# Pattern B's scores from stacked hi/lo operands in two fp32r passes, with a second key set where pattern C's position tables stand

## The chip, the cores and the metric

One core of one Trainium2 chip. The time is the device time of one execution in microseconds; the time before is the median of 3 runs.

## What is computed

A two-layer encoder trunk over 512 tokens of width 1024. In each layer one combined projection feeds four token mixers (A: windowed attention, B: differential attention, C: dilated attention, D: latent attention) and four gates; the gated branches are summed, projected and added, then comes a gated MLP. The change is in B, cut from the reference:

```python
def differential_attention(b_q, b_k, b_v, pos, q_norm, k_norm, lam_q1, ...):
    q = rms_norm(b_q.reshape(b, s, 2, B_HEADS, HEAD_DIM), q_norm)
    k = rms_norm(b_k.reshape(b, s, 2, B_HEADS, HEAD_DIM), k_norm)
    v = b_v.reshape(b, s, B_HEADS, B_V_DIM)
    ...
        sc = jnp.einsum('bqmhd,bsmhd->bmhqs', qblk, k, preferred_element_type=jnp.float32) * scale
        dist = jnp.abs(pblk[:, :, None] - posf[:, None, :])
        sc = sc - slopes[None, None, :, :, None, None] * dist[:, :, None, None]
        a = jax.nn.softmax(sc, axis=-1)
        a = a[:, 0] - lam[None, :, None, None] * a[:, 1]
        return jnp.einsum('bhqs,bshv->bqhv', a.astype(v.dtype), v, ...)
```

There are 4 heads with 2 maps each (head size 64), so with 4 query tiles of 128 tokens 32 score tiles of 128 x 512 in a layer.

## The kernel before, in words

Everything stays in SBUF; weights stream in through a two-deep buffer `raw` and are split by ScalarE into a high part `wh` (fp32r, L961) and by VectorE into the rest `wl` (L1481). Each dense product of TensorE is three fp32r matmuls, high by high, low by high, high by low (L579), six to a step. ORDER lists the dense blocks with their number of steps; it is the clock of the whole program. WINDOW gives each attention pattern a span of that clock, `slots` divides it into n + 4 slots, and every engine's program is a merge (`together`) of streams that yield the time at which they want to issue. So the order on each engine is fixed when the program is built, and semaphores do the rest.

B's window holds 32 steps in 36 slots between the blocks br0a and gate1b, so that of four slots three hold one dense step and one holds two. In a slot TensorE does, in this order: in odd slots the transposes of a mixed probability tile into bank TA (through L614), in even slots the product with the values into O1 (L850), and the scores of the step into the single bank S1 (L859). VectorE adds the bias and takes the minimum (L2023), ScalarE takes the exponential (L1366), VectorE mixes the two maps of a head (L2007, L2009, L2011), and the transposed tile is copied out of TA half by ScalarE (L1360), half by VectorE (L2017). TensorE may write the scores of the next step when L2023 has read S1.

The stationary operand of a score is `q_pad`, 128 rows of which 64 are the head's and 64 are zero; ScalarE copies q into it in eight pieces for a window, two copies each (L1307, `tiles_of`), pieces 0 and 1 before the window, piece p (2 to 7) after step 4p-4. The product is a plain fp32 one with kT.

Before the window, B's q and k are normalised and transposed, four tiles each: TensorE transposes a tile of 128 tokens into bank TD (`turn`), and `half_out` empties it, two of four column blocks by ScalarE (L1180 for k), two by VectorE (L1870). A's last steps run meanwhile, and their copy out of TA stands behind it on VectorE (L1978), A's output by heads is L2075, and its split for block br0a is ScalarE's L1189 and VectorE's L1878.

Pattern A does its scores in another way (`stacks_of_a`, `stacks`, L815): operands `q_two` with the high part of q in one half of the rows and a copy of it in the other, against keys kept twice. ScalarE writes the high part (L1324), VectorE copies it to the other rows (L1955) and writes the rest, q minus its high part (L1957).

`near` (second half) and `bias_c12` hold C's tables of position distances and masks; they are built once at the start and read in C's windows of both layers.

## Time and profile before

| | |
|---|---|
| median of 3 runs | 2708.42 us (2707.78 to 2709.2) |
| the profiled execution, time | 2709.8 us |
| its span, first to last instruction | 2708.0 us |
| granted TensorE clock, mean | 0.998 |
| TensorE busy | 2629.4 us, 97% |
| VectorE busy | 1639.1 us, 61% |
| ScalarE busy | 1231.4 us, 45% |
| B's score matmuls (L859), records and busy | 128, 66.4 us |
| DMA | 225.28 MB, mean 83 GB/s |

A plain fp32 matmul shows as two records. Matmuls are pipelined and their ends are modelled, so lengths of single ones overlap the next; distances between starts are the safer measure. ScalarE's and VectorE's lengths are their own.

### The profile page before, as it was taken

The numbers are of one execution on the slowest core, as the hardware profiler recorded it, in microseconds if no ns is written. First come the engines' busy times: TensorE is split into PE (matmuls) and PEld (weight loads), VectorE is DVE, ScalarE is ACT, GpSimd is POOL, SyncE is SP. The second block draws the span as 40 slices with busy tenths as digits, with TensorE's granted clock in tenths as the row PEclk, the third lists the DMA queues.
The fourth block names the chain that finished last, engine by engine and source line by source line (L and its number), as shares of the span: only waits on it lengthen the run. The fifth ranks groups of instructions, "written<-read, shape, count | busy, mean of one in ns | idle before, by whom it ended". The sixth has DMA issues, their size and how long they took to land. (4 is left out here: it accounts for less than half of the span.)

```text
span 2708.0 us, 36172 instructions
## 1 busy us (share of the span) xinstructions
PE 2629.4 (97%) x12982; PEld 2205.3 (81%) x12982; DVE 1639.1 (61%) x3432; ACT 1231.4 (45%) x2514; POOL 1.5 (0%) x6
## 2 busy tenths in 40 slices
PE   7999999999999999999999999999999999999999
PEld 6999987778877778888779998877788777888887
DVE  6554577545666647676664546775356566485665
ACT  5655545444544334333354555544445443443332
POOL 0000000000000000000000000000000000000000
PEclk9999999999999999999999999999999999999999
DMA  5212223222121332332332122221221213333332
GB/s 184 70 55 79 81 65 92 57 77 72 55 78 48 104 100 88 95 103 88 102 117 71 47 87 74 80 86 55 71 78 56 78 47 109 94 94 101 95 100 94
DMA packets 143874, 225.28 MB, mean 83 GB/s; under 512 B 15046, under 2 KB 69458, under 8 KB 142802
## 3 DMA queue, kind: packets, MB, share of 16 engines
q1 hardware_dynamic: 135842, 201.85, 24.8%
q10 hardware_dynamic: 7856, 21.12, 2.1%
q8 instruction: 106, 1.74, 0.3%
q14 instruction: 70, 0.57, 0.1%
HBM read 210.29 MB, written 12.65 MB: 82 GB/s over the span
## 5 line engine op out<-in xcount | busy, mean ns | idle before, releaser
L1481 DVE TENSOR_TENSOR s_wl<-s_raw,s_wh 128x1024 fp32r<-128x1024 f32 (+2 forms) x376 | 453.2, 1206 | 297.9 <-ACT s_wh L961 297.7
L961 ACT ACTIVATE s_wh<-s_raw 128x1024 fp32r<-128x1024 f32 (+2 forms) x376 | 392.0, 1043 | 396.6 <-PE bank L579 298.3
L579 PE MATMUL bank<-s_hTh,s_wh 128*128 128x512 f32 x1216 | 520.9, 428 | 1.6 <-DVE s_work L1839 1.6
L579 PE MATMUL bank<-s_hTh,s_wl 128*128 128x512 f32 x1216 | 474.7, 390 | 0.0
L579 PE MATMUL bank<-s_hTl,s_wh 128*128 128x512 f32 x1216 | 473.9, 390 | 0.0
L579 PE MATMUL bank<-s_wh,s_hTh 128*128 128x512 f32 (+1 forms) x1088 | 458.1, 421 | 4.5 <-DVE s_early L1621 3.4
L579 PE MATMUL bank<-s_wh,s_hTl 128*128 128x512 f32 (+1 forms) x1088 | 426.2, 392 | 0.0
L579 PE MATMUL bank<-s_wl,s_hTh 128*128 128x512 f32 (+1 forms) x1088 | 425.8, 391 | 0.0
L579 PEld LDWEIGHTS bank<-s_hTh,s_wh 128*128 128x128 f32 x1216 | 228.6, 188 | 69.8 <-issue 23.6
L1278 ACT ACTIVATE s_work<-s_work,s_stat 128x128 f32<-128x128 f32 (+3 forms) x320 | 167.5, 524 | 257.5 <-DVE s_work L2053 113.6
L579 PEld LDWEIGHTS bank<-s_hTl,s_wh 128*128 128x128 f32 x1216 | 228.9, 188 | 66.4 <-issue 24.4
L579 PEld LDWEIGHTS bank<-s_wh,s_hTh 128*128 128x128 f32 x1088 | 251.6, 231 | 34.6 <-issue 4.1
L579 PEld LDWEIGHTS bank<-s_wh,s_hTl 128*128 128x128 f32 x1088 | 251.7, 231 | 26.6
L579 PEld LDWEIGHTS bank<-s_wl,s_hTh 128*128 128x128 f32 x1088 | 253.4, 233 | 22.5 <-issue 0.5
L579 PEld LDWEIGHTS bank<-s_hTh,s_wl 128*128 128x128 f32 x1216 | 228.2, 188 | 49.1
L614 PE MATMUL bank<-s_consts,s_work 128*128 128x128 f32 (+1 forms) x1432 | 216.4, 273 | 16.0 <-DVE s_gTl L1878 8.9
L614 PEld LDWEIGHTS bank<-s_consts,s_work 128*128 128x128 f32 (+1 forms) x1432 | 172.6, 139 | 70.7 <-issue 34.3
L1978 DVE COPY s_work<-bank 128x128 f32<-128x128 f32 (+1 forms) x224 | 77.4, 345 | 207.4 <-PE bank L614 98.1
L579 PE MATMUL bank<-s_wh,s_gTh 128*128 128x512 f32 (+1 forms) x432 | 167.4, 387 | 5.6 <-ACT s_work L990 5.2
L579 PE MATMUL bank<-s_wl,s_gTh 128*128 128x512 f32 (+1 forms) x432 | 166.3, 385 | 0.0
L579 PE MATMUL bank<-s_wh,s_gTl 128*128 128x512 f32 (+1 forms) x432 | 166.2, 385 | 0.0
L579 PE MATMUL bank<-s_gTh,s_wh 128*128 128x512 f32 x256 | 111.4, 435 | 5.9 <-DVE s_gTl L1878 3.0
(202 smaller groups left out, 3408.4 us busy)
## 6 DMA issues: line engine op xcount, KB each, us to landing
s_raw<-in_w_in SPq DMA_DIRECT2D x168, 512.0 KB, 3.6
s_raw<-in_ffn_w_up SPq DMA_DIRECT2D x176, 256.0 KB, 3.1
s_raw<-in_ffn_w_down SPq DMA_DIRECT2D x44, 512.0 KB, 3.7
s_raw<-in_w_branch SPq DMA_DIRECT2D x32, 512.0 KB, 3.7
s_raw<-in_w_o SPq DMA_DIRECT2D x16, 512.0 KB, 3.7
x_keep<-s_work ACTq DMA_DIRECT2D x2, 2048.0 KB, 11.2
s_raw<-in_w_in SPq DMA_DIRECT2D x16, 256.0 KB, 3.0
gate_keep<-s_early ACTq DMA_DIRECT2D x4, 1024.0 KB, 4.3
```

Source lines behind the costliest of these rows:

```text
L579: last = mm(PJ[b][:, 0:width], st, mv, start=i == 0 and n == 1, stop=i == ntiles - 1 and n == 3 * chunks)
L614: last = nc.tensor.transpose(dst[0:m, (at + n) * P:(at + n) * P + k], src, ident[0:k, 0:k])
L961: a(wh[:, k % 3, 0:n], raw[:, s, 0:n], ACT.Copy).then_inc(*hi_split.up(own))
L1278: a(probs[:, u % 2, x0:x0 + w], scores[:, u % 2, x0:x0 + w], ACT.Exp, scale=-1.0, bias=stat[:, mins, c:c + 1], accum_out=stat[:, sums, c:c ...
L1481: v.tensor_tensor(wl[:, k % 3, 0:n], raw[:, k % 2, 0:n], wh[:, k % 3, 0:n].bitcast(F32), ALU.subtract).then_inc(*tile_split.up(own))
L1978: v.tensor_copy(probsT[:, u % 2, P * mid:P * hi], src[:, P * mid:P * hi]).then_inc(*ta_dve.up(own))
```

## The change

B's scores become two fp32r passes into the same bank. The stationary operands are `q_four`: for pass 0 the high part of q in the head's 64 rows and a copy of it in the other 64, for pass 1 the rest of q in the head's rows and zeros in the others. The moving operand `kB` has the high part of k in the head's rows and the rest of k in the other rows; as heads lie in pairs in the 128 rows, there is one such set for each half, so eight instructions of 64x512 on ScalarE (high part) and eight on VectorE (rest) take the place of four of 128x256 on each. The second set lies over C's tables. These go to DRAM after C's last step of layer 0, come back after B of layer 0, and layer 1's C waits for them. ScalarE's L1307 copies become copies into `q_four` (plus four that write the zeros), and VectorE gets `stacks_b`, two copies and two subtractions for each of eight pieces. TensorE waits for `q_stacked` in the place of `q_padded`, and the two passes signal once.

```diff
@@ -249,9 +249,10 @@
...
-    near = sb("near", [P, 2, NEAR])
+    with nc.sbuf_tensor("s_tables", [P, 2 * NEAR + 2 * SEQ], F32R) as tables:
+        pass
+    near, bias_c12 = sb("near", [P, 2, NEAR]), sb("bias_c12", [P, 2, SEQ])
...
-    bias_c12 = sb("bias_c12", [P, 2, SEQ])
@@ -289,6 +290,8 @@
...
+    kB = [t.rearrange("p (c n) -> p c n", c=4) for t in (stacked[:, AD + 2048:AD + 4096], tables[:, NEAR:NEAR + 2048])]
+    q_four = [t.rearrange("p (c h s n) -> p c h s n", c=2, h=2, s=2) for t in (stacked[:, 6144:7168], stacked[:, AD + 14336:AD + 15360])]
@@ -318,6 +321,8 @@
...
+    near_keep = nc.dram_tensor("near_keep", (P, NEAR), F32).ap()
+    bias_keep = nc.dram_tensor("bias_keep", (P, 2, SEQ), F32).ap()
@@ -853,10 +859,11 @@
...
-                        pe.wait_ge(*q_padded.at(l, n_pad[0] + pads_of("B", step)))
+                        pe.wait_ge(*q_stacked.at(l, 16 + pads_of("B", step)))
...
-                            mm(out, st, mv, start=start, stop=stop).then_inc(*s_ready.up())
+                            last = mm(out, st, mv, start=start, stop=stop)
+                        last.then_inc(*s_ready.up())
@@ -893,7 +900,8 @@
...
-                    return [(out[:], q_pad[:, n // 2, n % 2, :], kT[:, n // 2, :], True, True)]
+                    c = n // 2
+                    return [(out[:], q_four[c % 2][:, c // 2, n % 2, part, :], kB[n % 2][:, c, :], part == 0, part == 1) for part in range(2)]
@@ -1240,7 +1248,16 @@
...
-                yield from k_out(END["Bk"] + 6, kT, "bk")
+                for t in range(4):
+                    yield END["Bk"] + 6.4 + 2 * t
+                    src = group()
+                    for half in range(2):
+                        mine = slice(64 * half, 64 * half + 64)
+                        if l == 0 and t == 0 and half == 1:
+                            act.wait_ge(tables_moved, 16 * 2)
+                        act.wait_ge(*own.done(l))
+                        a(kB[half][mine, :, P * t:P * t + P], src[mine, :].rearrange("p (c n) -> p c n", c=4), ACT.Copy,
+                          scale=prm[mine, ROW["bk"]:ROW["bk"] + 1]).then_inc(*(td_act if half else act_step).up(own))
@@ -1338,14 +1355,34 @@
...
-                by_pair, by_map = (lambda g: slice(2 * g, 2 * g + 2)), (lambda g: slice(g, 4, 2))
+                def stacks_of_b():
+                    first, slot = done, slots("B")
+                    for piece in range(8):
+                        t, g = piece // 2, piece % 2
+                        yield slot[4 * piece - 4][1] + 0.8 * slot[0][2] if piece >= 2 else slot[0][1] - 6 + 3 * piece
+                        if piece == 0:
+                            act.wait_ge(*td_dve.at(l, B_HEADS - 4))
+                            act.wait_ge(*sq_used.at(l, sq_used.each))
+                        if piece:
+                            act.wait_ge(*s_ready.at(l, first + 4 * piece - 4 if piece >= 2 else first))
+                        if piece < 2:
+                            for half in range(2):
+                                other = slice(64 - 64 * half, 128 - 64 * half)
+                                act.wait_ge(*own.done(l))
+                                a(q_four[g][other, :, half, 1, :], q_pad[other, 0:2, half, :], ACT.Copy).then_inc(*q_zeroed.up(own))
+                        for half in range(2):
+                            mine = slice(64 * half, 64 * half + 64)
+                            act.wait_ge(*own.done(l))
+                            a(q_four[g][mine, :, half, 0, :], qT[mine, g:4:2, P * t:P * t + P], ACT.Copy).then_inc(*q_hi.up(own))
+
+                by_pair = lambda g: slice(2 * g, 2 * g + 2)
...
-                yield from tiles_of("B", qT, B_HEADS, by_map)
+                yield from stacks_of_b()
@@ -1391,6 +1428,11 @@
...
+                if l == 0:
+                    yield WINDOW["C2"][1] + 0.5
+                    act.wait_ge(*s_biased.at(l, 48))
+                    act.dma_start(near_keep, near[:, 1, :]).then_inc(tables_moved, 16)
+                    act.dma_start(bias_keep, bias_c12[:]).then_inc(tables_moved, 16)
@@ -1398,6 +1440,9 @@
...
+                if l == 0:
+                    act.dma_start(near[:, 1, :], near_keep).then_inc(tables_moved, 16)
+                    act.dma_start(bias_c12[:], bias_keep).then_inc(tables_moved, 16)
@@ -1922,7 +1967,14 @@
...
-                yield from k_out(END["Bk"] + 6, kT, "bk")
+                for t in range(4):
+                    yield END["Bk"] + 6.8 + 2 * t
+                    src = group()
+                    for half in range(2):
+                        mine, other = slice(64 * half, 64 * half + 64), slice(64 - 64 * half, 128 - 64 * half)
+                        dve.wait_ge(*own.done(l))
+                        v.scalar_tensor_tensor(kB[half][other, :, P * t:P * t + P], src[mine, :].rearrange("p (c n) -> p c n", c=4), prm[mine, ROW["bk"]:ROW["bk"] + 1],
+                                               kB[half][mine, :, P * t:P * t + P].bitcast(F32), ALU.mult, ALU.subtract).then_inc(*(td_dve if half else dve_step).up(own))
@@ -1956,6 +2008,22 @@
...
+
+            def stacks_b():
+
+                slot, n = slots("B"), 16
+                for piece in range(8):
+                    t, g = piece // 2, piece % 2
+                    yield (slot[4 * piece - 4][1] + 0.8 * slot[0][2] if piece >= 2 else slot[0][1] - 6 + 3 * piece) + 0.3
+                    for half in range(2):
+                        n += 1
+                        mine, other = slice(64 * half, 64 * half + 64), slice(64 - 64 * half, 128 - 64 * half)
+                        dve.wait_ge(*q_hi.at(l, n))
+                        dve.wait_ge(*own.done(l))
+                        v.tensor_copy(q_four[g][other, :, half, 0, :], q_four[g][mine, :, half, 0, :].bitcast(F32)).then_inc(*dve_step.up(own))
+                        dve.wait_ge(*own.done(l))
+                        v.tensor_tensor(q_four[g][mine, :, half, 1, :], qT[mine, g:4:2, P * t:P * t + P],
+                                        q_four[g][mine, :, half, 0, :].bitcast(F32), ALU.subtract).then_inc(*q_stacked.up(own))
@@ -2075,6 +2143,9 @@
...
+                if l:
+                    yield WINDOW["C0"][0]
+                    dve.wait_ge(tables_moved, 16 * 4)
```

How this moves VectorE's instructions, first where B's keys are transposed (layer 0). Before (L1870 is the key's half, L1978 the copy of A's probabilities, L2042 A's biasing, L2075 the output of A's last tile):

```order
L1870 TENSOR_SCALAR s_work<-bank,s_prm 128x2x128
L1978 COPY s_work<-bank 128x128
L1481 TENSOR_TENSOR s_wl<-s_raw,s_wh 128x1024
L1870 TENSOR_SCALAR s_work<-bank,s_prm 128x2x128
L1978 COPY s_work<-bank 128x128
L1870 TENSOR_SCALAR s_work<-bank,s_prm 128x2x128
L1481 TENSOR_TENSOR s_wl<-s_raw,s_wh 128x1024
L2071 TENSOR_TENSOR s_stat<-s_stat 128x8
L2073 RECIPROCAL s_stat<-s_stat 128x8
L2075 TENSOR_TENSOR s_work<-bank,s_stat 128x512
L1878 SCALAR_TENSOR_TENSOR s_gTl<-bank,s_gTh 128x4x128
```

Now (L1976 the rest of k, L2046 the copy, L2023 and L2025 `stacks_b`, L2143 the output, L1923 what block br0a waits for):

```order
L1976 SCALAR_TENSOR_TENSOR s_stacked<-bank,s_prm,s_stacked 64x4x128
L1976 SCALAR_TENSOR_TENSOR s_tables<-bank,s_prm,s_tables 64x4x128
L1526 TENSOR_TENSOR s_wl<-s_raw,s_wh 128x1024
L2139 TENSOR_TENSOR s_stat<-s_stat 128x8
L2141 RECIPROCAL s_stat<-s_stat 128x8
L2143 TENSOR_TENSOR s_work<-bank,s_stat 128x512
L2023 CAST s_stacked<-s_stacked 64x2x128
L2025 TENSOR_TENSOR s_stacked<-s_work,s_stacked 64x2x128
L2023 CAST s_stacked<-s_stacked 64x2x128
L2025 TENSOR_TENSOR s_stacked<-s_work,s_stacked 64x2x128
L1923 SCALAR_TENSOR_TENSOR s_gTl<-bank,s_gTh 128x4x128
```

This begins with the fourth key tile. Each key tile has two instructions of 64x512 instead of one of 128x256; piece 0 of the stacks stands right ahead of these rows, and piece 1 ahead of L1923.

Second, VectorE in B's window around piece 3 (layer 0). Before (L2023 biasing, L2007 to L2011 mixing, L2017 the copy of the transposed probabilities):

```order
L2007 RECIPROCAL s_stat<-s_stat 128x1
L2009 SCALAR_TENSOR_TENSOR s_stat<-s_stat,s_lam 128x1
L2011 SCALAR_TENSOR_TENSOR s_work<-s_work,s_stat 128x512
L2023 ISA s_work,s_stat<-bank,s_bias_b 128x512
L2023 ISA s_stat 128x1
L2017 COPY s_work<-bank 128x256
L2023 ISA s_work,s_stat<-bank,s_bias_b 128x512
L2023 ISA s_stat 128x1
```

Now (L2091 biasing, L2075 to L2079 mixing, L2085 the copy):

```order
L2077 SCALAR_TENSOR_TENSOR s_stat<-s_stat,s_lam 128x1
L2079 SCALAR_TENSOR_TENSOR s_work<-s_work,s_stat 128x512
L2091 ISA s_work,s_stat<-bank,s_bias_b 128x512
L2091 ISA s_stat 128x1
L2023 CAST s_stacked<-s_stacked 64x2x128
L2025 TENSOR_TENSOR s_stacked<-s_work,s_stacked 64x2x128
L2023 CAST s_stacked<-s_stacked 64x2x128
L2025 TENSOR_TENSOR s_stacked<-s_work,s_stacked 64x2x128
L2085 COPY s_work<-bank 128x256
L2091 ISA s_work,s_stat<-bank,s_bias_b 128x512
L2091 ISA s_stat 128x1
```

The block of four stands right ahead of the copy that TensorE's product with the values needs; pieces 2 to 7 all have it there.

## Rows read from the trace of the kernel before

**Rows 1.** The page, busy times of the engines, and ScalarE's weight split.

```profile
PE 2629.4 (97%) x12982; PEld 2205.3 (81%) x12982; DVE 1639.1 (61%) x3432; ACT 1231.4 (45%) x2514; POOL 1.5 (0%) x6
...
L961 ACT ACTIVATE s_wh<-s_raw 128x1024 fp32r<-128x1024 f32 (+2 forms) x376 | 392.0, 1043 | 396.6 <-PE bank L579 298.3
```

**Rows 2.** Windows: busy (x) of PE, PEld, DVE, ACT, POOL, clock, DMA, GB/s.

```profile
792.00:808.00 16.00, 14.81 (x67) 10.08 (x66) 13.75 (x29) 6.37 (x15) 0.00 (x0) 1.00 0.15 37
808.00:822.00 14.00, 14.00 (x67) 10.43 (x66) 8.03 (x21) 6.43 (x16) 0.00 (x0) 1.00 0.22 73
```

**Rows 3.** Timeline of TensorE, 808 to 823 us: start, length, line.

```profile
809.77 1.02 PE L859 MATMUL bank<-s_work,s_q_pad 128*128 128x512 f32 x2
...
812.46 1.02 PE L859 MATMUL bank<-s_work,s_q_pad 128*128 128x512 f32 x2
...
813.55 0.40 PE L579 MATMUL bank<-s_hTl,s_wh 128*128 128x512 f32 x1
...
814.69 1.05 PE L850 MATMUL bank<-s_work 128*128 128x128 f32 x8
```

**Rows 4.** Timeline of TensorE in A's window: stacked scores, dense after.

```profile
701.91 0.59 PE L815 MATMUL bank<-s_stacked 128*128 128x384 f32 x2
...
702.57 0.40 PE L579 MATMUL bank<-s_wl,s_hTh 128*128 128x512 f32 x1
```

**Rows 5.** Timeline of ScalarE, 811 to 814 us: q copies.

```profile
812.65 0.86 ACT L1307 ACTIVATE s_q_pad<-s_work 64x256 f32<-64x256 f32 x2
```

**Rows 6.** Timeline of VectorE, 811 to 814.5 us.

```profile
811.01 0.69 DVE L2023 CUSTOM_DVE_ANT_0 s_work<-bank,s_bias_b 128x512 f32<-128x512 f32 x1 [1.63 <-PE bank L859]
...
814.01 0.42 DVE L2017 COPY s_work<-bank 128x256 f32<-128x256 f32 x1 [2.30 <-issue]
```

**Rows 7.** Timelines of VectorE and TensorE, where TensorE waited for the copy.

```profile
799.46 0.42 DVE L2017 COPY s_work<-bank 128x256 f32<-128x256 f32 x1 [0.98 <-ACT s_work L1360]
...
800.03 1.13 PE L850 MATMUL bank<-s_work 128*128 128x128 f32 x8 [0.25 <-DVE s_work L2017]
```

**Rows 8.** Timelines of ScalarE and VectorE, one piece of A's stacks.

```profile
658.12 0.87 ACT L1324 ACTIVATE s_stacked<-s_work 64x256 fp32r<-64x256 f32 x2
...
658.57 0.29 DVE L1955 CAST s_stacked<-s_stacked 64x256 fp32r<-64x256 f32 x1 [0.99 <-ACT s_stacked L1324]
...
660.08 0.28 DVE L1978 COPY s_work<-bank 128x128 f32<-128x128 f32 x1
```

**Rows 9.** Timelines of ScalarE, VectorE and TensorE while B's keys are transposed.

```profile
762.98 0.45 ACT L1180 ACTIVATE s_work<-bank,s_prm 128x256 f32<-128x256 f32 x1
...
763.47 0.48 DVE L1870 TENSOR_SCALAR s_work<-bank,s_prm 128x256 f32<-128x256 f32 x1 [1.22 <-ACT s_work L1180]
763.87 0.28 DVE L1978 COPY s_work<-bank 128x128 f32<-128x128 f32 x1
...
773.89 0.48 DVE L1870 TENSOR_SCALAR s_work<-bank,s_prm 128x256 f32<-128x256 f32 x1 [3.19 <-ACT s_work L1180]
...
776.05 0.69 DVE L2075 TENSOR_TENSOR s_work<-bank,s_stat 128x512 f32<-128x512 f32 x1
...
765.00 0.82 PE L614 MATMUL bank<-s_consts,s_work 128*128 128x128 f32 x6
...
768.88 0.82 PE L614 MATMUL bank<-s_consts,s_work 128*128 128x128 f32 x6
...
777.77 0.60 PE L614 MATMUL bank<-s_consts,s_work 128*128 128x128 f32 x4
779.87 0.47 PE L579 MATMUL bank<-s_gTh,s_wh 128*128 128x512 f32 x1 [1.50 <-DVE s_gTl L1878]
```

**Rows 10.** Lines L1189 and L1878: ns min/median/max, first and last start.

```profile
L1189 ACT ACTIVATE s_gTh<-bank,s_gain x8: 687/689/692, 911.9 to 2264.7; 128x512 fp32r<-128x512 f32 x8
...
L1878 DVE SCALAR_TENSOR_TENSOR s_gTl<-bank,s_gain,s_gTh x8: 750/751/753, 913.0 to 2265.5; 128x512 fp32r<-128x512 f32 x8
```

**Rows 11.** DMA issues: engine, times, KB each, us to landing.

```profile
gate_keep<-s_early ACTq DMA_DIRECT2D x4, 1024.0 KB, 4.3
```

More of the change, by code:

```diff
@@ L123 @@
     pj_dve=108, sq_used=60, normed=53, combined=4, sublayer_normed=4, h_normed=2, h_scaled=2, rstd=3, rows_turned=1, rows_out=1, conv_done=44, td_ready=77, td_act=77, td_dve=77, nt_ready=16, nt_act=24,
-    nt_dve=24, ta_ready=128, ta_act=128, ta_dve=128, q_padded=48, q_hi=16, q_stacked=16, q_zeroed=2, s_ready=144, s_biased=144, p_ready=144, b_mixed=16, o_ready=128, o_out=24,
+    nt_dve=24, ta_ready=128, ta_act=128, ta_dve=128, q_padded=32, q_hi=32, q_stacked=32, q_zeroed=6, s_ready=144, s_biased=144, p_ready=144, b_mixed=16, o_ready=128, o_out=24,
     gains_in=1, ssum=16, lam_dot=1, lam_exp=1, c_diff=2, c_exp=2, merged_sum=24, merged_hi=8, merged_lo=8, conv_mid=44,
-    e_ready=22, hidden_val=22, hidden_hi=22, hidden_lo=22, act_step=189, dve_step=534, params_in=16, direct_in=8,
+    e_ready=22, hidden_val=22, hidden_hi=22, hidden_lo=22, act_step=193, dve_step=554, params_in=16, direct_in=8,
     x_moved=2, c0_moved=6, gates_moved=4,
@@ L168 @@
 B_NORM = WINDOW["B"][1]
-PADS = dict(C0=16, C1=8, C2=8, B=16)
+PADS = dict(C0=16, C1=8, C2=8)
 def pads_of(name, u):
@@ L390, in _build @@
     pad_clear = sem("pad_clear")
+    tables_moved = sem("tables_moved")
     nc.disable_value_cache = True
@@ L911, in attentions @@
                                      heads_in(57, 72) + [q_zeroed.at(l, 2)], keys=near_keys, tile_of=out_tiles)
-                yield from attention_b(b_scores, heads_in(B_HEADS, 96))
+                yield from attention_b(b_scores, heads_in(B_HEADS, 96) + [q_zeroed.at(l, 6)])
             return norm1(), dense(), turns(), attentions()
@@ L2084, in attentions @@
                 yield from attention_b()
-            return norm1(), dense(), turns(), stacks(), attentions(), c_combine()
+            return norm1(), dense(), turns(), stacks(), stacks_b(), attentions(), c_combine()
         together(setup_first(), setup_rest(), splits(), *[shifted(stream, TOTAL * l) for l in range(DEPTH) for stream in layer(l)])
```

## The prediction

> **What bounds the kernel now.** First the page's busy times: TensorE is busy 2629.4 us of a span of 2708.0 [rows 1]. That looks as if any TensorE time saved were time won, so the next thing to read is who keeps TensorE fed in the places that the change touches. The change touches two stretches of each layer: B's attention window (about 782 to 892 us in layer 0, again in layer 1), and the 20 us before it, in which B's keys are transposed. The windows show that in the calm part of B VectorE has room (8.03 of 14 us) [rows 2]. What is short is not an engine's time but the way from one step to the next, so I read the timelines of the three engines side by side and measured distances between starts, since the ends of matmuls are modelled.
>
> **The matmul itself.** A score of B is one fp32 product of 128x512 that shows as two records. From its start at 812.46 to the second dense matmul after it at 813.55 are 1.09 us; one dense fp32r matmul of 512 columns takes 0.23 us from start to start (the same rows in the timeline repeat it hundreds of times), so a score holds TensorE 0.87 us [rows 3]. Pattern A already does what B will do, two fp32r passes over stacked operands: with 384 columns, from 701.91 to 702.57, 0.66 us, less 0.23, is 0.43 [rows 4]. B has 128 columns more in each pass, at the granted clock of 1.00 (2.4 GHz) 2 x 0.053 us: 0.54. So a score saves 0.33 us, and 32 scores in each of two layers 21.1 us. That is the ceiling. The Trainium skill (FP8 and Floating Point Precision, TensorE Precision Notes) says true fp32 takes four passes through the array; with one for each fp32r product the saving would be two passes of 512 columns, 0.43 us a score and 27 us in all. The rows have 0.1 us more in A's pair than its columns, so I take 0.33.
>
> **What B's window gives back.** The second order listing shows the price: once in four steps VectorE now gets a block of four small instructions (two copies, two subtractions) just ahead of its copy of the transposed probabilities (L2017, now L2085). It happens for pieces 2 to 7, six times a layer. The distance from a score of step 4p-4 to the product with the values in step 4p-2 is a chain: score to biasing on VectorE 1.24 us (809.77 to 811.01), on to ScalarE's q copy 1.64 (812.65), on to VectorE's copy of the probabilities 1.36 (814.01) [rows 3, 5, 6], and at least 0.57 from there to the product, as in the place where TensorE waited for it (799.46 to 800.03) [rows 7]. That is 4.81, and TensorE needed 4.92 (809.77 to 814.69): the cover is 0.11 us. After the change the first link is 0.91 (0.33 less), the second stays, and the third is as in A: first q copy on ScalarE to first stacking copy 0.45 (658.12 to 658.57), the block 1.51 (658.57 to 660.08) [rows 8]. 0.91 + 1.64 + 0.45 + 1.51 + 0.57 = 5.08. TensorE alone would want 4.92 - 0.66 = 4.26, since two scores lie in between. So each piece makes TensorE wait about 0.82 us; six are 4.9 us a layer.
>
> More goes where VectorE is full. While a block of the branch projection comes out (about 792 to 808) it is busy 13.75 of 16 us, and TensorE already waits there [rows 2]; 1.51 us of stacking make 15.3. TensorE's demand would be 16 less its waits of 1.2 and less five scores of 0.33, 13.2. Laying VectorE's instructions in the new order, each as late as its releaser, I get about 1.1 us lost there beyond the 0.82, the same at the second such stretch (862 to 878), and 1.4 for the four other groups, where the mixing of the two maps or the evacuation of the output now comes last. That is an estimate from the same rows, 3.6 us. B's window then gives 10.6 - 4.9 - 3.6 = **2.1 us a layer**, out of 10.6.
>
> **What the keys cost.** One PSUM bank (TD) takes all transposes of heads, so TensorE's next one waits until ScalarE and VectorE have both emptied it. Before, each took one half: 128x256, ScalarE at 762.98, VectorE at 763.47, and the copy of A's probabilities behind it on VectorE at 763.87 [rows 9]. Now each does two instructions of 64x512, and the second engine needs the first one's result. The nearest rows with a gain and 512 columns are 0.689 us on ScalarE and 0.751 on VectorE [rows 10]; with 0.03 for each wait in a row the pairs are 1.41 and 1.53. First tile: ScalarE still begins at 762.98, VectorE at 764.4, the bank is free at 765.95; TensorE wanted it at 765.00 and gets it at 766.05: **1.05 us**. Second tile: A's last biasing is behind VectorE's pair and so 2.0 us late, then come exp, a weight split (1.04 us, [rows 1]) and the pair on ScalarE, from 768.25, then VectorE's, to 771.2; TensorE wanted the bank at 768.88 + 1.05 and gets it at 771.35: **1.4**. Third tile: no wait, the next transpose is due 3.9 us later. Fourth: ahead of it ScalarE now has piece 0 of the stacks, two zero copies and two q copies (four at 0.43, by 0.86 for two [rows 5]) and the split, so its pair starts at about 776.4, VectorE's at 777.85; from there to the heads of A's last tile were 2.16 us (773.89 to 776.05), now 3.2 with the longer pair, 781.05, and the transpose of that tile is ready 0.75 later, at 781.8. TensorE wanted it at 777.77 + 2.45: **1.6**. Behind it, piece 1 of the stacks (1.51) stands before the instruction for which the branch block br0a waits, in a wait that was 1.5 us already (779.87): another **0.15** [rows 9]. Sum 4.2 us a layer, on TensorE's path, with nothing that pays it back.
>
> **At no cost:** ScalarE's four q copies before the first score leave (L1307), but TensorE didn't wait for them. The tables' two stores (layer 0, after C's last step) and two loads (after B) are DMA issues on ScalarE's queue; the nearest row, a 1 MB store of gates, lands in 4.3 us [rows 11], the stores have over 300 us until B's keys and the loads hundreds until layer 1's first biasing. If an issue did delay a weight split, it would be by under 1 us, four times: -0 to +3 us. Without their cover that is the whole price.
>
> **The sum.** Per layer -2.1 + 4.2 = +2.1, twice +4.2. The profiled execution took 2709.8 us, so 2714.0; the median of the runs shown is 1.4 lower: **2712.6 us**, 0.15% slower. A measurement of this kernel can tell about 0.2% (5.4 us) from no change, so the forecast is "within 0.2%".
>
> **Rivals.**
> *TensorE's columns decide (faster).* If the blocks of four find gaps that I don't see and the key pairs overlap better, the losses are halved: of 21.1 us B's window gives back 8.5 and the keys take 4.2 (both layers together), -8.4, 2700 us; without losses it would be 2687. For it: 97% busy [rows 1], and nearly no waits. Against it: the cover of 0.11 us in [rows 3, 5, 6]. It decides if the block takes under about 1 us. The Trainium skill (VectorE: DVE Perf Modes, "The TRN2 errata") has each instruction that reads SBUF pay a fixed cost and asks for tiles of 512 elements or more. By that rule, the trace agrees: four instructions of 256 elements take 1.51 us [rows 8], one of 512 with two operands 0.75 [rows 10]. It speaks for the next rival.
> *The transposes' bank decides (slower).* The keys are on the path as worked out, 8.4 us in both layers, and B gives nothing since VectorE's queue, with 1.51 us more in six of eight groups, sets the pace throughout: 2716.8; if the full stretches lose 1.5 us a layer more, 2720. It decides from the point where a group of four steps saves under 0.66 us. For it: the 13.75 of 16 us [rows 2].
> *The passes aren't cheaper (slower).* If a stacked pass took what a record takes now (0.43), 21 us of gain would go: 2734. Against it: A's pair [rows 4].
> *The tables come late.* Then the first key tile of layer 0 waits tens of us; 300 us of lead speak against it.
>
> **Chances.** Forecast (within 5.4 us) 0.44; transposes' bank and VectorE's queue, slower by more, 0.36, passes or tables another 0.03; faster by more, 0.17. The range reaches from 2700, the case of halved losses, to 2720, the second rival's far end, and takes in the 3 us of the DMA issues; it leaves out less than 0.1 on each side.
>
> **What would show it.** Profile after: the new score pair about 0.54 us by start distances; TensorE's idle in B's window waiting for the copy of probabilities (now L2085), six times a layer, 0.5 to 1 us each; between 762 and 785 us transposes waiting for VectorE's key instruction (L1976), 1 to 1.5 us twice; VectorE's block of four 1.5 us. If B's window (first score to last) is shorter by over 6 us, the block is better hidden than I say; if the stretch before it isn't longer by 3 to 5 us, my key chain is wrong; waits on a DMA of the tables would break the claim of no cost.

## The result, and the profile after

| | before | after |
|---|---|---|
| median | 2708.73 us (2707.78 to 2709.2, 5 runs) | 2722.84 us (2721.16 to 2724.29, 5 runs) |
| ratio | | 1.0052, interval 1.0040 to 1.0064 |
| profiled execution, its span | 2709.8, 2708.0 us | 2723.67, 2721.8 us |
| granted TensorE clock, mean | 0.998 | 0.994 |

The change makes the kernel 14.1 us slower. The forecast was 2712.6 in a range of 2700 to 2720, with 0.44 on "within 0.2%": the time is outside the range, on the slow side.

The busy times of the page after answer to [rows 1]:

```profile
PE 2617.5 (96%) x12982; PEld 2210.4 (81%) x12982; DVE 1670.7 (61%) x3504; ACT 1243.8 (46%) x2530; POOL 1.5 (0%) x6
...
L969 ACT ACTIVATE s_wh<-s_raw 128x1024 fp32r<-128x1024 f32 (+2 forms) x376 | 391.9, 1042 | 391.9 <-PE bank L585 297.9
```

TensorE shows 11.9 us less busy time and the span is 13.8 us longer, so it idles 25.7 us more. Where it idles, the view of TensorE's waits says (us in total, times, longest). First before:

```profile
PE bank L859 <- DVE s_stat L2023: 3.1, 4, 0.8
PE bank L579 <- DVE s_gTl L1878: 3.0, 2, 1.5
...
PE bank L850 <- DVE s_work L2032: 1.5, 2, 0.8
...
PE bank L850 <- DVE s_work L2017: 1.1, 4, 0.3
```

And after:

```profile
PE bank L856 <- DVE s_work L2085: 13.4, 12, 1.4
...
PE bank L620 <- DVE s_tables L1976: 5.3, 4, 1.6
...
PE bank L585 <- DVE s_gTl L1923: 3.9, 2, 1.9
PE bank L620 <- DVE s_work L2143: 3.7, 2, 1.9
PE bank L865 <- DVE s_stat L2091: 3.7, 4, 0.9
...
PE bank L856 <- DVE s_work L2100: 2.9, 2, 1.5
PE bank L620 <- DVE s_work L2079: 2.6, 5, 0.7
```

The first line is the copy of B's probabilities behind the block of four: twelve waits, six a layer, where the forecast had put them. The next ones (L1976, L1923, L2143) are the key stretch. Against the lines of before that makes 12.3 us more at the copy (L2017, 1.1 us there) and 9.9 more in the key stretch (L1878, 3.0), 22 of the 25.7 us.

Waits are not yet time of the kernel, since part of them is paid by the cheaper scores. For that I numbered the dense matmuls of the one line that issues them (L579, now L585; 8976 in each trace), and subtracted the start of the same one in the two traces: how far the changed kernel is behind (+) or ahead (-). The first column is the place, in us of the kernel before; the other columns are kernels of the experiments, explained there. Each column rests on one execution.

| at | after | keys only | cheap keys | passes only | block earlier | overlap only | last |
|---|---|---|---|---|---|---|---|
| 762.0, before B's keys | -1.3 | -0.1 | -0.1 | -0.2 | -0.1 | -0.7 | +1.4 |
| 779.9, product behind them | +4.4 | +4.2 | -0.1 | -0.2 | +5.5 | +3.0 | +3.3 |
| 783.2, at B's first scores | +7.2 | +4.2 | -0.1 | -0.2 | +7.1 | +4.6 | +3.3 |
| 900.2, behind B | +6.1 | +4.8 | -0.6 | -5.4 | +1.8 | +4.2 | -1.9 |
| 2108.1, layer 1 | +7.1 | +2.6 | -1.7 | -6.7 | +2.7 | +3.8 | -2.1 |
| 2125.5 | +12.5 | +6.7 | -1.7 | -6.7 | +8.1 | +7.3 | -0.5 |
| 2128.1 | +14.0 | +6.6 | -1.7 | -6.7 | +9.6 | +9.5 | -0.6 |
| 2250.1 | +13.6 | +6.6 | -2.1 | -12.0 | +4.2 | +10.1 | -5.4 |
| 2700.1 | +13.9 | +6.4 | -2.6 | -11.8 | +4.1 | +10.4 | -5.5 |

Read downwards, the column "after" has the whole result: +5.7 and +5.4 us in the two key stretches, then +2.8 and +1.6 in the few us behind them, and only -1.1 and -0.4 in the two windows of B.

The +2.8 behind the keys was not in the forecast. Windows of after, with columns as in [rows 2] (the clock is the 0.50):

```profile
779.80:783.50 3.70, 0.66 (x5) 0.42 (x4) 3.14 (x9) 2.43 (x6) 0.00 (x0) 1.00 0.54 139
783.50:790.30 6.80, 6.04 (x14) 4.79 (x15) 1.84 (x2) 1.04 (x1) 0.00 (x0) 0.50 0.28 79
790.30:792.00 1.70, 1.70 (x9) 1.33 (x8) 0.70 (x2) 0.52 (x1) 0.00 (x0) 0.99 0.00 0
```

After 3.7 us in which TensorE worked 0.66, its granted clock is at the lower of its two levels (1.2 in the place of 2.4 GHz) for 6.8 us, and the dense matmuls start 0.43 us apart, not 0.23, as the timeline of TensorE shows:

```profile
784.26 0.77 PE L585 MATMUL bank<-s_gTh,s_wh 128*128 128x512 f32 x1 [1.93 <-DVE s_gTl L1923]
784.83 0.63 PE L585 MATMUL bank<-s_gTl,s_wh 128*128 128x512 f32 x1
785.25 0.63 PE L585 MATMUL bank<-s_gTh,s_wl 128*128 128x512 f32 x1
```

Such stretches, each 3.41 us or twice that, stand at three places in the trace of before (402.9, 662.3, 1375.7 us; a fourth begins behind its last matmul) and at eight of after (346.6, 783.5, 1380.8, 1698.3, 1756.3, 2015.7, 2138.6, 2230.8 us), nine lengths in all. The comparison has a step at each. One length costs 1.4 to 1.6 us where TensorE is the path, 0.7 at 346.6 and 1698.3; the 1.4 at 1756.3 is made up again within 20 us. The one at 2230.8 lies in B's window of layer 1; in layer 0, without it, the same place moves by 0.8 us less and the whole window by 0.7 less, so I put it at 0.7. The sum against before: -1.3 us ahead of B's keys in layer 0, +2.8 and +1.6 behind the two key stretches, +0.7 in layer 1's window, and +0.7, -0.2 and +1.6 at 1698.3, 1756.3 and 2015.7, places that the change does not touch. That is about +6 us of the 13.9, +5.1 of it in the stretches that the change touches.

### The profile page after: what moved, and what is told of

It reads as the page before. It is cut to its first block and busy times, and to the rows that moved or that the text cites. A ratio compares the mean times of both kernels' runs of the same rounds, so it can differ in the third digit from the quotient of the medians.

```text
span 2721.8 us, 36316 instructions
## 1 busy us (share of the span) xinstructions
PE 2617.5 (96%) x12982; PEld 2210.4 (81%) x12982; DVE 1670.7 (61%) x3504; ACT 1243.8 (46%) x2530; POOL 1.5 (0%) x6
## 5 line engine op out<-in xcount | busy, mean ns | idle before, releaser
L585 PE MATMUL bank<-s_hTh,s_wh 128*128 128x512 f32 x1216 | 504.4, 415 | 1.4 <-DVE s_work L1884 1.4
L585 PE MATMUL bank<-s_hTh,s_wl 128*128 128x512 f32 x1216 | 474.8, 390 | 0.0
L585 PE MATMUL bank<-s_hTl,s_wh 128*128 128x512 f32 x1216 | 474.4, 390 | 0.0
L585 PE MATMUL bank<-s_wh,s_hTh 128*128 128x512 f32 (+1 forms) x1088 | 458.8, 422 | 5.1 <-DVE s_early L1666 3.3
L585 PE MATMUL bank<-s_wh,s_hTl 128*128 128x512 f32 (+1 forms) x1088 | 426.6, 392 | 0.0
L585 PE MATMUL bank<-s_wl,s_hTh 128*128 128x512 f32 (+1 forms) x1088 | 426.0, 392 | 0.0
L585 PEld LDWEIGHTS bank<-s_wh,s_hTh 128*128 128x128 f32 x1088 | 252.1, 232 | 35.1 <-issue 4.1
L585 PEld LDWEIGHTS bank<-s_hTh,s_wh 128*128 128x128 f32 x1216 | 228.8, 188 | 61.3 <-issue 14.6
L585 PEld LDWEIGHTS bank<-s_hTl,s_wh 128*128 128x128 f32 x1216 | 229.1, 188 | 58.0 <-issue 14.4
L585 PEld LDWEIGHTS bank<-s_wh,s_hTl 128*128 128x128 f32 x1088 | 251.9, 232 | 26.6
L585 PEld LDWEIGHTS bank<-s_wl,s_hTh 128*128 128x128 f32 x1088 | 253.9, 233 | 22.6 <-issue 0.5
L585 PEld LDWEIGHTS bank<-s_hTh,s_wl 128*128 128x128 f32 x1216 | 228.5, 188 | 49.1
L620 PE MATMUL bank<-s_consts,s_work 128*128 128x128 f32 (+1 forms) x1432 | 216.8, 273 | 26.2 <-DVE s_gTl L1923 8.6
L620 PEld LDWEIGHTS bank<-s_consts,s_work 128*128 128x128 f32 (+1 forms) x1432 | 171.7, 139 | 83.8 <-issue 39.1
L2046 DVE COPY s_work<-bank 128x128 f32<-128x128 f32 (+1 forms) x224 | 77.4, 345 | 208.0 <-PE bank L620 98.8
L585 PE MATMUL bank<-s_wh,s_gTh 128*128 128x512 f32 (+1 forms) x432 | 167.5, 388 | 5.4 <-ACT s_work L998 5.1
L585 PE MATMUL bank<-s_wh,s_gTl 128*128 128x512 f32 (+1 forms) x432 | 166.2, 385 | 0.0
L585 PE MATMUL bank<-s_wl,s_gTh 128*128 128x512 f32 (+1 forms) x432 | 166.1, 385 | 0.0
L1283 ACT ACTIVATE s_work<-bank 128x256 f32<-128x256 f32 (+1 forms) x224 | 78.1, 349 | 83.8 <-PE bank L620 82.5
```

Source lines behind the costliest of these rows:

```text
L585: last = mm(PJ[b][:, 0:width], st, mv, start=i == 0 and n == 1, stop=i == ntiles - 1 and n == 3 * chunks)
L620: last = nc.tensor.transpose(dst[0:m, (at + n) * P:(at + n) * P + k], src, ident[0:k, 0:k])
L1283: a(probsT[:, u % 2, P * lo:P * mid], src[:, P * lo:P * mid], ACT.Copy).then_inc(*ta_act.up(own))
L2046: v.tensor_copy(probsT[:, u % 2, P * mid:P * hi], src[:, P * mid:P * hi]).then_inc(*ta_dve.up(own))
```

## The experiments

The kernel before was timed again beside the experiments: 2709.16 us beside the first four, 2708.22 beside block earlier, keys overlapped and both, 2709.91 beside the last two. Each ratio is to the one beside it. Times that are compared with the changed kernel's 2722.84 carry such shifts of up to 1.7 us.

**Keys only.** The kernel before, with each bank of B's keys emptied in two instructions of 64x512 on each engine, VectorE behind ScalarE as in the change. Scores, q copies and everything else as before.

```diff
-                yield from k_out(END["Bk"] + 6, kT, "bk")
+                    for half in range(2):
+                        a(kT[mine, ...], src[mine, :], ACT.Copy, scale=...)
...
+                        v.scalar_tensor_tensor(kT[mine, ...], src[mine, :], prm[mine, ...], kT[mine, ...], ALU.mult, ALU.max)
```

> The kernel before with only the key part added: ScalarE writes kT in two pieces of 64x512 for each tile, VectorE reads the same PSUM bank again in two pieces of 64x512 and writes the same values; scores stay plain fp32. Theory 1 (the TD bank's turnover costs TensorE directly): the traces show 5.7 and 5.4 us a layer for keys plus pieces 0 and 1; without those pieces some 4.5 to 5 us a layer, so +9 to +10 us, and one to three stretches of 3.41 us at half clock more than before (1.7 us each at most): 2718 to 2723. Rival (the keys hide, the loss is the clock and the scores' window): within 3 us of before, the mean clock as before.

Measured: 2717.02 us (2715.41 to 2720.9, 9 runs), ratio 1.0030 (1.0021 to 1.0040). Column "keys only": +4.3 and +4.1 us at the keys, and the clock does not fall near them. The time is 1 us under theory 1's range, whose +4.5 to +5 us a layer were a little too much. So the double key evacuation alone costs 8 us in both layers, about what I forecast for it within the change (8.4). Within the change the stretch costs 11; what comes on top there are the stacks of pieces 0 and 1. The wait by the key instruction is as in after:

```profile
PE bank L614 <- DVE s_work L1938: 5.3, 4, 1.6
...
PE bank L614 <- DVE s_work L2089: 1.9, 2, 1.0
```

**Cheap keys.** The changed kernel with one key set, emptied as before; all scores use it.

```diff
-   kB[n % 2][:, c, :]
+   kB[0][:, c, :]
...
-                    for half in range(2): ...
+                    half_out(lambda c0, c1: kB[0][:, c0:c1, P * t:P * t + P], same=prm[:, ROW["bk"]:ROW["bk"] + 1])
```

> The changed kernel with the key part undone: each engine again writes one 128x256 half of a key tile, into the first key set, which all scores read (the second set and the rest of the keys are left out, so the scores are not B's). Everything else of the change stays. Theory 1: 10 to 11 us less than the changed kernel by the key chain, less 0.5 to 1 us for pieces 0 and 1 that stay on the path, and the low-clock stretches near the keys go too: 2708 to 2713. Rival: within 3 us of the changed kernel (2720 to 2724).

Measured: 2707.53 us (2705.05 to 2709.27, 11 runs), ratio 0.9995 (0.9987 to 1.0004); 15.3 us less than after. That is half a us under theory 1's range. The key stretch costs 0.0 in both layers, though pieces 0 and 1 are still stacked there. But B gives only 0.5 and 0.4 us a layer with all 64 scores cheap (each window has a stretch at half clock inside, some 0.7 us), and the copy makes TensorE wait as long as in after (13.4 us in twelve). So with the keys out of the way the change is worth next to nothing: VectorE's block takes most of what the window could give, as the next run shows.

**Passes only.** As cheap keys, and VectorE's block of four is left out for pieces 2 to 7 as well.

```diff
-                for piece in range(8):
+                for piece in range(2):
```

> The two fp32r passes alone: keys as in the cheap-keys version, and VectorE's block of four left out for pieces 2 to 7 (the low part of q and its copy stay those of pieces 0 and 1, so the scores are not B's). What is left is the ceiling. Theory 1: 64 scores times 0.33 us less than the kernel before, less 1 to 3 us for the pieces ahead of the window and waits that come out: 2688 to 2692. Rival (a pass costs more than A's, or the mixing of the two maps bounds the step): 2696 or more.

Measured: 2700.21 us (2698.05 to 2702.21, 5 runs), ratio 0.9968 (0.9955 to 0.9980). I had expected 2688 to 2692: missed, the rival's bound of 2696 held. B gives 5.2 us a layer in both layers, not the 10.6. TensorE's timeline shows the new score:

```profile
807.48 1.05 PE L856 MATMUL bank<-s_work 128*128 128x128 f32 x8
808.28 0.71 PE L865 MATMUL bank<-s_stacked 128*128 128x512 f32 x2
808.83 0.39 PE L585 MATMUL bank<-s_hTh,s_wh 128*128 128x512 f32 x1
809.06 0.39 PE L585 MATMUL bank<-s_hTl,s_wh 128*128 128x512 f32 x1
...
810.20 0.60 PE L620 MATMUL bank<-s_consts,s_work 128*128 128x128 f32 x4
810.55 0.71 PE L865 MATMUL bank<-s_stacked 128*128 128x512 f32 x2
...
811.34 0.40 PE L585 MATMUL bank<-s_hTl,s_wh 128*128 128x512 f32 x1
```

The score takes 809.06 - 808.28 - 0.23 = 0.55 us, where 0.54 was forecast. But the instruction ahead of it is shorter too. Transposes and score together, to the second dense matmul, took 1.53 us (812.02 to 813.55 in before) and take 1.14 (810.20 to 811.34). Product with the values and score took 1.99 (808.88 to 810.87) and take 1.58 (807.48 to 809.06). So a score saves about 0.40 us, 12.8 a layer, and of these even a window without the block gives back 5.2. What takes the rest is in the waits of TensorE in this run:

```profile
PE bank L856 <- DVE s_work L2075: 5.4, 8, 0.9
...
PE bank L865 <- DVE s_stat L2081: 3.2, 4, 0.8
PE bank L620 <- DVE s_work L2069: 3.1, 7, 0.7
PE bank L856 <- DVE s_work L2090: 2.9, 2, 1.4
```

These are 14.6 us in both layers. In before the same places have 5.7 (3.1, 1.5 and 1.1, none by the mixing). They lie along the way of one step through three engines (score, biasing, exp, mixing, transposes, copy, product), so I take this way to be what B's window waits for once the score is cheap. No run shortened one of its links.

**Block later.** The changed kernel with VectorE's block moved behind the next biasing (step 4p-3), so that the copy of the probabilities no longer stands behind it.

```diff
-   ... else slot[0][1] - 6 + 3 * piece) + 0.3
+   ... else slot[0][1] - 6 + 3 * piece) + (0.7 if piece >= 2 else 0.3)
```

> The changed kernel; only VectorE's block of four for pieces 2 to 7 moves behind the biasing of its step, so that it no longer stands ahead of the copy of the transposed probabilities. The result is B's in full. Theory 1: TensorE's 13.4 us of waits for that copy fall to 1 to 3 us, and the gain of the cheaper scores appears: 8 to 13 us less than the changed kernel, 2710 to 2715. Rival (VectorE is simply full in B's window, the place of the block doesn't matter): other waits take the place of these, under 3 us less.

Measured: 2734.13 us (2731.61 to 2735.38, 4 runs), ratio 1.0091 (1.0077 to 1.0105). Missed, and in the wrong direction: 11 us slower than after. The wait by the copy fell as expected, and a longer one came up:

```profile
PE bank L620 <- DVE s_work L2079: 17.0, 14, 2.3
...
PE bank L856 <- DVE s_work L2085: 5.4, 8, 0.9
```

L2079 is the mixing of the two maps, and the transposes (L620) wait for it. The block had moved from ahead of one link of the chain to ahead of another. The trace also has twelve stretches at half clock, so not all of the 11 us is the move. B's window of layer 0, with one of the twelve inside it, makes the kernel 4.0 us later, where after won 1.1.

**Block earlier.** Passes only and block later lead to one question: where does the step chain leave VectorE and ScalarE idle? In the changed kernel ScalarE waits 1.4 to 3.6 us for the biasing of step 4p-4 before the exp that stands ahead of its q copies. VectorE, in the kernel before, was idle for 2.30 us behind that biasing (811.01 and 814.01 in [rows 6]). So ScalarE's q copies went ahead of the exp, and VectorE's block right behind the biasing of step 4p-4. The run does not tell the two moves apart.

```diff
-   yield slot[4 * piece - 4][1] + 0.8 * slot[0][2] if piece >= 2 ...
+   yield slot[4 * piece - 4][1] + 0.06 * slot[0][2] if piece >= 2 ...
...
-   yield (slot[4 * piece - 4][1] + 0.8 * slot[0][2] if piece >= 2 ...) + 0.3
+   yield slot[4 * piece - 4][1] + 0.25 * slot[0][2] if piece >= 2 ...
```

> The changed kernel with the stacking of pieces 2 to 7 placed earlier: ScalarE's two q copies stand ahead of the exp of the step (in the run before they had ScalarE idle for 1.9 to 2.8 us there) and VectorE's block of four right behind the biasing of step 4p-4, where VectorE was idle for about 2.3 us. The same work, nothing left out. Theory one (the score evacuation of the step chain is held up only by where the block stands; 13.4 us of TensorE waits by the copy in the changed kernel): the window of pattern B gains like the run without the block, about -5 us a layer in the place of -1.1 and -0.4, so 8 to 10 us less than the changed kernel: 2712 to 2715, and 2 to 4 less again if stretches at half clock go with the waits. Theory two (VectorE and ScalarE have no room at any place of the step): the wait moves to the mixing or the transposes as it did when the block was put later, and the time is within 3 us of the changed kernel (2720 to 2726) or above it.

Measured: 2713.70 us (2711.77 to 2715.7, 11 runs), ratio 1.0018 (1.0010 to 1.0027); 9.1 less than after, in theory one's range. B gives 5.3 us a layer in both layers, the same as with the block left out. Timeline of VectorE in this run:

```profile
798.07 0.42 DVE L2085 COPY s_work<-bank 128x256 f32<-128x256 f32 x1 [2.16 <-issue]
...
802.80 0.68 DVE L2091 CUSTOM_DVE_ANT_0 s_work<-bank,s_bias_b 128x512 f32<-128x512 f32 x1
...
803.59 0.29 DVE L2023 CAST s_stacked<-s_stacked 64x256 fp32r<-64x256 f32 x1
...
804.76 0.42 DVE L2025 TENSOR_TENSOR s_stacked<-s_work,s_stacked 64x256 fp32r<-64x256 f32 x1
```

The block still takes its 1.6 us; what it no longer does is stand between a result of another engine and the copy that passes it on. The wait by the copy halves, to 6.9 us in six:

```profile
PE bank L856 <- DVE s_work L2085: 6.9, 6, 1.4
```

**Keys overlapped.** The changed kernel with a semaphore for ScalarE's first half, so that VectorE starts on its first half while ScalarE does its second; and the stacks of pieces 0 and 1 put behind the key copies.

```diff
-   .then_inc(*(td_act if half else act_step).up(own))
+   .then_inc(*(td_act if half else k_half).up(own))
...
-                    src = group()
+                        dve.wait_ge(*(td_act.at(l, n_turn[0]) if half else k_half.at(l, t + 1)))
...
-   ... else slot[0][1] - 6 + 3 * piece
+   ... else slot[0][1] - (4.4, 0.9)[piece]
```

> The changed kernel with the two key copies of one PSUM bank overlapped: VectorE starts on its first half when ScalarE has finished its first, not when it has finished both, and the stacking of pieces 0 and 1 is put behind the key evacuations. The same work, nothing left out. Theory one (the +5.5 us a layer of the key stretch are the serial chain ScalarE 2 x 0.69, then VectorE 2 x 0.75, at each of four banks): the chain shortens by about 0.7 us a bank, and the key stretch falls from +5.5 to +2 to +3.5 us a layer: 2716 to 2719, and 1.6 to 3 less if the stretch at half clock at 783.5 us goes too. Theory two (most of it is the stacking and hi_out standing in VectorE's queue, or the stretch at half clock alone): within 2 us of the changed kernel, 2721 to 2725.

Measured: 2722.66 us (2720.81 to 2723.09, 5 runs), ratio 1.0047 (1.0033 to 1.0061). Theory one missed, theory two's time was right. But "the overlap gives nothing" is not what the trace shows. The key waits fell from 5.3 to 2.7 us, the one of the branch block from 3.9 to 3.0, and the one for the division rose from 3.7 to 4.9. The key stretches cost +4.6 and +4.3 us in the place of +5.7 and +5.4, but the trace has eleven lengths at half clock in the place of nine. In the timeline of TensorE:

```profile
766.52 0.85 PE L621 MATMUL bank<-s_consts,s_work 128*128 128x128 f32 x6 [0.51 <-DVE s_tables L1979]
...
771.54 0.84 PE L621 MATMUL bank<-s_consts,s_work 128*128 128x128 f32 x6 [0.97 <-DVE s_tables L1979]
...
783.08 0.77 PE L621 MATMUL bank<-s_consts,s_work 128*128 128x128 f32 x4 [2.47 <-DVE s_work L2146]
```

The first two are 0.7 us shorter than in after (1.19 and 1.62), as expected. The third, 1.87 in after, is 2.47: L2146 is the division of A's last tile, and my own move of piece 0 had put that piece between the last key copy and the division.

**Both.** Block earlier and keys overlapped in one kernel.

> Both edits in one kernel, the whole computation: earlier stacking of pieces 2 to 7 and overlapped key copies. If both theories one hold, the gains add: 8 to 10 and 4 to 7 below the changed kernel, 2705 to 2711, at or just below the kernel before (2709). If half-clock stretches return to the number that the kernel before has (3), 2698 to 2706. If only one of the two holds, 2712 to 2719.

Measured: 2713.58 us (2709.57 to 2715.31, 11 runs), ratio 1.0017 (1.0008 to 1.0026): as a time, only one of the two held, and 2713.58 lies in the range given for that. The key stretches cost +4.5 and +4.2 us, 1.1 us a layer less than in block earlier, and B gives 5.4 and 4.8. But this run has ten lengths at half clock, four of them (two double stretches) right behind the keys, where block earlier has seven and two.

**Overlap only.** The overlap of the key copies with pieces 0 and 1 where the change has them, to tell the two edits of "keys overlapped" apart.

> The changed kernel with the overlap of the two key copies alone: VectorE starts on its first half when ScalarE has finished its first; the stacking of pieces 0 and 1 stays where the changed kernel has it. The same work, nothing left out. Theory one (the overlap is worth about 0.65 us at each of the banks for which TensorE waits, and what the run before gave back came from the stacking of piece 0, which stood ahead of the division of the last tile, 2.47 us of wait): the key stretch up to the product of the last normed tile costs about +3.5 us a layer in the place of +5.7 and +5.4, and the time is 2717 to 2720. Theory two (the overlap itself gives nothing, because what was late is late for another reason): within 2 us of the changed kernel, 2721 to 2725.

Measured: 2718.28 us (2714.75 to 2721.86, 9 runs), ratio 1.0029 (1.0019 to 1.0039); 4.6 less than after, in theory one's range. Column "overlap only": the keys cost +3.7 and +3.5 us. The overlap works; the moved piece had hidden it.

**Last: the division first.** Both edits, and on VectorE the division of the last tile ahead of the fourth key copy and of piece 0. In the trace of both, its input was ready at about 775 us and VectorE was idle until 775.41, but the division began at 780.95.

```diff
-                    yield END["Bk"] + 6.8 + 2 * t
+                    yield END["Bk"] + 6.8 + 2 * t + (1 if t == 3 else 0)
...
-   ... slot[0][1] - (4.4, 0.9)[piece] + 0.3
+   ... slot[0][1] - (2.5, 0.9)[piece] + 0.3
```

> Overlapped key copies, the earlier stacking of pieces 2 to 7, and on VectorE the division of the last tile ahead of the fourth key copy and of the stacking of piece 0 (in the run with both edits TensorE waited 2.47 us a layer for that division, whose input had been ready since the products at 774.5 us, while VectorE stood idle). The same work, nothing left out. Theory one (the order on VectorE is what costs in this stretch): the wait by the division goes, the key stretch costs +2 to +3 us a layer in the place of +4.6 and +4.2, and the time is 2706 to 2710, level with the kernel before (2708); 1.6 us less for each stretch at half clock that goes. Theory two (the wait moves to the low part of the normed tile or to the first scores): 2712 to 2715, as the run with both edits (2713.6).

Measured: 2703.79 us (2701.83 to 2705.29, 6 runs), ratio 0.9972 (0.9961 to 0.9983), against a before of 2709.91. With the change whole, nothing left out, it is 19 us faster than the changed kernel and 6 faster than the one before. The timeline of VectorE shows the new order:

```profile
775.99 1.23 DVE L1527 TENSOR_TENSOR s_wl<-s_raw,s_wh 128x1024 fp32r<-128x1024 f32 x1 [0.41 <-ACT s_wh L970]
...
777.76 0.69 DVE L2146 TENSOR_TENSOR s_work<-bank,s_stat 128x512 f32<-128x512 f32 x1
778.55 0.74 DVE L1979 SCALAR_TENSOR_TENSOR s_stacked<-bank,s_prm,s_stacked 64x512 fp32r<-64x512 f32 x1
```

TensorE's wait for the division is gone. Left in this stretch of the timeline of TensorE are the two short key waits and the wait that the kernel before has too (1.50 at 779.87, [rows 9]):

```profile
783.13 0.47 PE L586 MATMUL bank<-s_gTh,s_wh 128*128 128x512 f32 x1 [1.50 <-DVE s_gTl L1924]
```

The clock stays up there, as the windows show:

```profile
780.00:792.00 12.00, 10.49 (x50) 8.11 (x48) 7.80 (x19) 7.11 (x14) 0.00 (x0) 1.00 0.18 54
```

The keys cost +1.9 and +1.6 us, B gives 5.2 and 4.8, and in the whole trace there are five lengths at half clock, not nine. The time came out 2 us under theory one's range.

## Why the prediction was wrong

By the forecast's own steps:

- **The saving of a score** was put at 0.33 us, and is about 0.40. The new pair was right (0.55 for 0.54), but the old record's price was taken from its own start, and part of it lay in the instruction ahead. The estimate of 0.43 from the four-pass rule of the Trainium skill (FP8 and Floating Point Precision, TensorE Precision Notes), which the forecast set aside, is nearer to the run than my 0.33. It would have raised the ceiling of 21.1 us; no run gave back more than 5.4 us a layer of it.
- **The stall at the copy** was the right mechanism in the right place, twelve times, and mis-sized: 0.82 us forecast, 13.4 / 12 = 1.1 measured.
- **B's window** as a sum, -2.1 us a layer: measured -1.1, and -0.4 with a stretch at half clock inside it that takes some 0.7. Without the clock that is -2.3 for both layers in the place of -4.2.
- **The keys**, +4.2 us a layer: measured +5.7 and +5.4. The three key waits were 1.19, 1.62 and 1.87 us (forecast 1.05, 1.4, 1.6), the wait of the branch block 0.43 longer (forecast 0.15). That is 5.1 by waits, and the matmul behind each wait is a little longer too (0.85 for 0.82 at the transposes). Each term is there; the first three measured 13 to 17% more than forecast, the last three times as much. Keys only tells the parts apart: it has the first two waits as after has them (5.3 us in four), but 0.98 us a layer by the division in the place of 1.87, and 1.5 at the branch block in the place of 1.93. So, by difference, the stacks of pieces 0 and 1 (ScalarE's copies for them included) cost 1.3 us a layer. The one term that is theirs alone, the 0.15, is the one undervalued most.
- **Nothing for the clock** is the step that failed by most. The forecast has no term for it: it took the granted clock of 1.00 in both stretches for given and gave no reason why it should stay there. It is about +6 us of the 13.9. The terms that were there, with their sizes put right (2.6 us more for the keys, 1.9 less for B), give 2717.1; the forecast with the clock alone added gives 2718.5. Each is still within the range. The two together give 2723.0, so it took both, and the clock is the larger.
- **DMA issues at no cost** held. Passes only has stores and loads as in the change and is at -0.2 us in front of B, with no wait on them. The DMA issues of after:

```profile
near_keep<-s_near ACTq DMA_DIRECT2D x1, 640.0 KB, 3.9
s_near<-near_keep ACTq DMA_DIRECT2D x1, 640.0 KB, 10.8
bias_keep<-s_bias_c ACTq DMA_DIRECT2D x1, 512.0 KB, 5.0
s_bias_c<-bias_keep ACTq DMA_DIRECT2D x1, 512.0 KB, 12.3
```

Of the rivals, the second (the transposes' bank, with no gain from B) came nearest: its 2716.8 to 2720 holds the 2717.1 of the trace without the clock. The first (TensorE's columns decide) needed gaps for the block that I did not see. They exist, but not where the change had put it: block earlier has found them. The block did not have to be shorter for that: it takes 1.6 us there. In this rival's sum B's window *loses* 8.5 us (and so gives back 12.6), and the keys take 4.2: the -8.4 is right, the words are not. Its comparison of four instructions of 256 elements (1.51 us) with one of 512 (0.75) does not show that small instructions are dear, since twice 0.75 is as much for the same 1024 elements. The subtractions do: 0.42 us for 256 elements (L2025 of after), 0.69 for 512 (L1669).

What lets the clock fall stays open. Over all executions the changed kernel has the lower clock: its five show a mean of 0.994 to 0.996, the 19 of the kernel before beside the first experiments 0.996 to 0.999. In those 19 the time goes with it: 2711.30 and 2712.82 us at 0.996, 2707.79 and 2705.18 at 0.999. A difference of 0.003 over 2709 us is some five lengths (an estimate from these numbers). So the same kernel differs by several lengths from one execution to the next, and each trace is one execution. The counts of lengths at half clock are 3 in before, keys only and passes only, 5 in the last kernel, 7 in cheap keys and block earlier, 8 in overlap only, 9 in after, 10 in both, 11 in keys overlapped and 12 in block later.

Beside the keys of layer 0 they suggest that the waits let it fall: 1.87 and 1.93 us idle around 0.66 of work and 6.8 us at half clock (after), 2.47 and 1.50 and again 6.8 (keys overlapped, both), 1.24 and 1.93 and 3.4 us (overlap only, table row 783.2 against 779.9: +1.6), 0.98 and 1.51 and none (keys only), 1.50 alone and none (before, cheap keys, last). But block earlier and block later have the waits of after there and only 3.4 us, and so has after itself in layer 1. Cheap keys has more stretches than before without any wait by the keys. And at 344.8 us, where the change has done nothing yet, before and after have the same wait, and only after has the fall. Timelines of TensorE and windows, before and after:

```profile
344.84 1.08 PE L803 MATMUL bank<-s_work 128*128 128x64 f32 x8 [1.76 <-DVE s_work L2062]
346.60:350.00 3.40, 3.40 (x25) 3.33 (x24) 3.16 (x17) 1.15 (x6) 0.00 (x0) 1.00 0.00 0
...
344.83 1.08 PE L809 MATMUL bank<-s_work 128*128 128x64 f32 x8 [1.78 <-DVE s_work L2130]
346.60:350.00 3.40, 3.40 (x13) 3.25 (x12) 3.16 (x17) 1.15 (x6) 0.00 (x0) 0.50 0.00 0
```

So a wait alone does not decide it, and no run varied an idle time alone.

## What to carry to other kernels

Extra work for an engine with 39% idle time costs nothing or everything, depending on what it stands in front of. Against the window without them, the same four instructions (six times a layer) cost 4 to 5 us a layer ahead of the copy and 9 or more ahead of the mixing, stretches at half clock included. Right behind the biasing of step 4p-4, with ScalarE's q copies moved too, they cost nothing. Before adding a block, list for each engine which of its instructions hands a result to the next engine in a step, and put the block behind the one whose successor takes longest to come back. When a PSUM bank is emptied by two engines in series, signal each piece by itself, and look at what is queued behind. And where a change makes TensorE idle in a kernel that is 97% busy, widen the range by what the rows show for stretches at the lower clock (here 1.4 to 1.6 us for each 3.41 us on TensorE's path), since the count differs between executions of one kernel.

## What the runs showed of the hardware that was not expected

- Instructions on half of the partitions are no cheaper: the 64x512 key copies of after, below, take 0.69 and 0.74 us, the 128x512 ones in [rows 10] 0.689 and 0.751. Two of them for a bank take 1.4 us, and the two on VectorE 1.5, where one of 128x256 was 0.45 and 0.48 [rows 9]. From the timelines of ScalarE and VectorE of after:

```profile
761.90 0.69 ACT L1259 ACTIVATE s_stacked<-bank,s_prm 64x512 fp32r<-64x512 f32 x1
...
763.39 0.74 DVE L1976 SCALAR_TENSOR_TENSOR s_stacked<-bank,s_prm,s_stacked 64x512 fp32r<-64x512 f32 x1 [2.41 <-ACT s_tables L1259]
```

- The granted clock falls to half in stretches of 3.41 us, or of 6.83, in all eleven traces, three to twelve lengths in a span of 2700 us. The same wait of 1.8 us is followed by a fall in one trace and by none in another.
- Start distances show part of the price of an fp32 matmul of two records in the instruction ahead of it: eight small products with the values (L850, L856), then a score, take 1.99 us to the second dense matmul with fp32 and 1.58 with two fp32r passes, 0.41 for a score whose own starts show 0.32.
